# A pair of products ahead of the last logits, and a weight load that waits for the rows' stores

## What is computed

```python
u = rmsnorm(h, norm_ffn_g[i])                         # normalised rows
aff = softmax(einsum('nd,de->ne', xf, router_w))      # xf: the rows u; router's logits
gate, idx = lax.top_k(aff.T, cap)                     # each expert's 64 tokens
xs = xf[idx]                                          # its rows, gathered
hid = silu(einsum('ecd,edf->ecf', xs, w_gate)) * einsum('ecd,edf->ecf', xs, w_up)
out = einsum('ecf,efd->ecd', hid, w_down) * gate[..., None]
```

## Time and profile before

| what | value |
|---|---|
| executions | 1513.92, 1514.42, 1514.67 us (median 1514.42) |
| the profiled execution | 1513.21 us, of which the span is 1511.4 us |
| TensorE busy | 1496.6 us (99% of the span) |
| VectorE, ScalarE, GpSimd busy | 1335.3, 1283.8, 443.9 us |
| read from and written to memory | 473.70 and 20.97 MB, 327 GB/s over the span |
| granted TensorE clock, mean | 0.998 of full speed |

### The profile page before, as it was taken

One profiled execution on the slowest core, in us unless ns is written; L12 is line 12 of the kernel. 1 busy time (PEld: TensorE's weight loads), 2 busy tenths in 40 slices (PEclk: granted clock), 3 DMA queues, 4 the chain that ended last, 5 costly groups with the idle time before them and its releaser, 6 DMA issues.

```text
span 1511.4 us, 21957 instructions
## 1 busy us (share of the span) xinstructions
PE 1496.6 (99%) x7514; PEld 1212.0 (80%) x7514; DVE 1335.3 (88%) x1415; ACT 1283.8 (85%) x1611; POOL 443.9 (29%) x354
## 2 busy tenths in 40 slices
PE   9999999999999999999999999999999999999997
PEld 8888888878864888888888888888888888888876
DVE  7776887787864999999999999999999999999988
ACT  6777766676653799999999999999999999999997
POOL 0434203252222224232332423224232322520103
PEclk9999999999999999999999999999999999999999
DMA  9615447333575999999999999999999999999998
GB/s 351 210 71 179 150 166 267 98 126 126 188 260 217 399 420 393 416 401 398 410 403 410 394 407 401 396 412 397 409 392 396 413 397 407 397 410 382 391 394 345
DMA packets 156023, 498.57 MB, mean 330 GB/s; under 512 B 11008, under 2 KB 36736, under 8 KB 155968
## 3 DMA queue, kind: packets, MB, share of 16 engines
q1 hardware_dynamic: 144624, 461.54, 77.9%
q0 software_dynamic: 10048, 34.22, 7.4%
q10 hardware_dynamic: 1296, 2.10, 0.4%
HBM read 473.70 MB, written 20.97 MB: 327 GB/s over the span
## 4 chain that ended last, share of the span: by engine, by line
PE 82%; ACT 5%; DVE 5%; issue 3%; DMA 2%; POOL 2%; SPq 0%; POOLq 0%; ACTq 0%; DVEq 0%
PE ps L2124 71%; PE ps L2173 4%; PE ps L2180 2%; ACT w_high L1286 2%; POOL arena L746 2%; DVE w_rest L1437 1%; ACT arena L950 1%; PE ps L2442 1%; PE ps L2224 1%; DMA raw<-w_gate 1%; PE ps L2290 1%; DVE arena L1511 1%; ACT arena L1257 1%; DVE arena L1534 1%; DMA u_rows<-arena 1%
## 5 line engine op out<-in xcount | busy, mean ns | idle before, releaser
L1437 DVE TENSOR_TENSOR w_rest<-raw,w_high 128x2048 fp32r<-128x2048 f32 x212 | 479.9, 2294 | 36.9 <-ACT w_high L1286 25.1
L1286 ACT CAST w_high<-raw 128x2048 fp32r<-128x2048 f32 x184 | 352.1, 1915 | 17.6 <-PE ps L2124 14.7
L2124 PE MATMUL ps<-w_high,xt_high 128*128 128x512 f32 x984 | 305.2, 390 | 0.7 <-DVE w_rest L1437 0.6
L2124 PE MATMUL ps<-w_rest,xt_high 128*128 128x512 f32 x984 | 304.3, 389 | 0.0
L2124 PE MATMUL ps<-w_high,xt_rest 128*128 128x512 f32 x984 | 304.3, 389 | 0.0
L2124 PEld LDWEIGHTS ps<-w_high,xt_high 128*128 128x128 f32 x984 | 184.1, 188 | 41.6 <-DVE w_rest L1437 2.4
L1437 DVE TENSOR_TENSOR w_rest<-early,w_high 128x2048 fp32r<-128x2048 f32 x90 | 204.4, 2287 | 13.4 <-ACT w_high L1286 13.3
L2124 PEld LDWEIGHTS ps<-w_high,xt_rest 128*128 128x128 f32 x984 | 184.7, 188 | 38.5
L2124 PEld LDWEIGHTS ps<-w_rest,xt_high 128*128 128x128 f32 x984 | 184.7, 188 | 38.4
L1437 DVE TENSOR_TENSOR w_rest<-raw_more,w_high 128x2048 fp32r<-128x2048 f32 x92 | 206.0, 2275 | 4.7 <-ACT w_high L1286 4.7
L870 POOL DMA_INDIRECT h_rows<-xh,rows x15 | 109.2, 7280 | 303.8 <-ACT xh L1268 303.8
(11 more groups left out here) (323 smaller groups left out, 2471.3 us busy)
## 6 DMA issues: line engine op xcount, KB each, us to landing
raw<-w_down SPq DMA_DIRECT2D x64, 1024.0 KB, 9.1
raw<-w_gate SPq DMA_DIRECT2D x62, 1024.0 KB, 8.0
raw<-w_up SPq DMA_DIRECT2D x62, 1024.0 KB, 9.8
raw_more<-w_down SPq DMA_DIRECT2D x32, 1024.0 KB
early<-w_down SPq DMA_DIRECT2D x32, 1024.0 KB, 8.0
raw_more<-w_gate SPq DMA_DIRECT2D x31, 1024.0 KB
raw_more<-w_up SPq DMA_DIRECT2D x31, 1024.0 KB
early<-w_gate SPq DMA_DIRECT2D x31, 1024.0 KB, 9.9
```

The lines of the kernel that those rows point to most:

```text
L1286: nc.scalar.copy(w_high[:, i % SLOTS, :], src).then_inc(high_done, 1)
L1437: nc.vector.tensor_tensor(w_rest[:, j, :], src, w_high[:, j, :].bitcast(F32), ALU.subtract).then_inc(rest_done, 1)
L2124: done = nc.tensor.matmul(out, lhs, rhs, start=start and part == 0, stop=stop and part == 2)
```

## The change

Two edits. On TensorE, the pair of products for share 0 of piece 0 leaves its place behind `last_group` and is issued between the last `quarter_logits` and the last `logits` of trunk 1, with the waits that stood ahead of it. On SyncE, piece 1 of `load_second` waits for the stores of the normalised rows as well, a wait that piece 2 had; piece 2 keeps its wait for the gather.

```diff
@@ load_second(i), SyncE
                     sp.wait_ge(scaled, TILES * TRUNKS)
                     sp.wait_ge(h_out, 16 * TILES * TRUNKS)
+                    sp.wait_ge(u_out, 16 * TILES * TRUNKS)
                 elif i == 2:
 
-                    sp.wait_ge(u_out, 16 * TILES * TRUNKS)
                     sp.wait_ge(gathered, 16)
@@ last_group(b), TensorE
                 quarter_logits(b, 3)
                 if b + 1 < TRUNKS:
                     project_t(b + 1, None, "q0", pair_number(b + 1, "q", 0), KC // 2)
+                else:
+                    first_early_gate_up(b)
                 logits(b, 3)
@@ new
+            def first_early_gate_up(b):
+
+                pe.wait_ge(early_xt_done, 1)
+                wait_copied(pe, b, GROUPS - 1, "o6")
+                wait_copied(pe, b, GROUPS - 1, "o7")
+                early_gate_up(0, (0,))
@@ behind the groups, TensorE
-            pe.wait_ge(early_xt_done, 1)
-            wait_copied(pe, TRUNKS - 1, GROUPS - 1, "o6")
-            wait_copied(pe, TRUNKS - 1, GROUPS - 1, "o7")
-            early_gate_up(0)
+            early_gate_up(0, (1,))
             early_gate_up(1, (0,))
             turn_lists(1)
             early_gate_up(1, (1,))
```

## The result

The changed kernel takes 1516.56 us at the median of 22 executions (1514.17 to 1518.50, but for one at 1659.57, whose mean granted clock was 0.85 and which is left out of the ratio). The kernel before took 1513.97 us beside it (22 executions, 1513.41 to 1516.07). The ratio is 1.0014 (by the medians alone 1.0017), with a 95% interval of 1.0007 to 1.0020: the change makes the kernel slower, by 2.6 us at the medians. Forecast were 1513.8 us in a range that ended at 1515.4. The profiled execution of after took 1517.09 us (1515.2 of span), that of before 1513.21.

A forecast was written before the change was run, and what follows sets the result against it. TensorE, busy 1496.6 of 1511.4 us, was taken as the bound, so only its two waits (1.16 us) could yield. Rows 0.65 us earlier, 0.2 of it from the pair, made 1514.42 into 1513.8; range 1512.6 to 1515.4.

The forecast's parts named there:

- Part 1: Pair of products moved into TensorE's 0.46 us hole before the last logits: logits 0.55 us late, lists turned 0.2 us earlier.
- The stores' end: Stores of the normalised rows, freed of the w_up load, finish their last 0.33 MB in 0.8 us and signal at 455.3.
- The third rival: Stores' tail is slow for its own reason, landing near 457 even without the load; 1514.2 us, chance 0.07.
- The gather's releaser: First expert's gather is released by the row numbers at 456.6, not by the stores, and starts 0.5 us later at 457.1.
- The gather's delay: The w_up load overlaps the first expert's gather by about 1 us and delays it by 0.3 us.
- a row and a rule: Gather beside load: profile row shows a queue's tail hardly moving (0.06 MB beside 0.75); skill's rule says queues alternate by packet.
- the sum: Load issued near 455.4, gather started 457.1, TensorE on the rows 0.65 us earlier: 1513.21 becomes 1512.6, at the median 1513.8.
- The second rival: The w_up load starves the first expert's gather: 0.3 us slower (1514.7), at worst 3.6 us (1518.1); chance 0.12.
- Hidden work: ScalarE's cast of the w_up load slips 1 to 4 us, hidden because its products come 23 us behind.
- the likeliest case: TensorE takes up the gathered rows at 461.4 instead of 462.05; gain 0.65 us, between 0.3 and 1.05, chance 0.55.
- The base of the sum: Median of the measured executions of the kernel before, 1514.42 us, from which the gain of 0.65 was subtracted.
- the ends: Outcomes bounding the whole-kernel forecast: 1513.3 us with a gain of 1.05, 1514.7 us with a loss of 0.3.

The follow-up runs named there:

- e8: Changed kernel, with the w_up load waiting until GpSimd has asked for the gather, instead of for the stores; 1517.50 us, ratio 1.0029 to the kernel before.
- e4: Changed kernel plus four pairs of unused products on TensorE just ahead of its wait for the gathered rows; 1514.32 us, ratio 1.0007 to the kernel before.
- e5: The changed kernel itself, run again beside other runs on the same chip; 1516.04 us, ratio 1.0017 to the kernel before.
- e2: Kernel before, with only the w_up load's added wait for the stores of normalised rows, the pair left in place; 1515.29 us, ratio 1.0011.
- e9: Changed kernel, with the 1 MB w_up load issued as four 256 KB loads one behind the other; 1516.89 us, ratio 1.0021 to the kernel before.
- e3: Changed kernel, with the w_up load waiting for the gather instead of the stores; 1513.08 us, ratio 1.0000 to the kernel before.
- e1: Changed kernel, with the pair moved but the w_up load given back its old wait; 1513.07 us, ratio 0.9998 to the kernel before.
- e6: Changed kernel, with the second half of the w_up load waiting for the gather to land; 1513.56 us, ratio 1.0002 to the kernel before.
- e7: Kernel before, with the w_up load waiting for the gather and the pair left in place; 1512.96 us, ratio 0.9998.

## Why the prediction was wrong

- **Part 1 was right.** The logits stand 1.73 us behind the quarter logits (1.81 was worked out), VectorE's scaling now waits for them, for 0.18 us, and the lists gain 0.2 us. This is VectorE's timeline, to set against the earlier trace rows:

```profile
441.52 0.22 DVE L1896 TENSOR_TENSOR lg<-ps,rstd 128x64 f32<-128x64 f32 x1 [0.18 <-PE ps L2489]
...
457.36 0.15 DVE L1838 TENSOR_TENSOR first_rows_at<-topt 64x1 uint32<-64x1 f32 x1
```

- **The stores' end was mis-sized by 1.5 us.** The step took the last 0.33 MB of the stores at their full rate, 0.8 us. Measured from the last store's issue, they land 9.46 us behind it instead of 10.02, where the prediction had about 8.0 (455.3 less 447.29). The row of 0.06 MB in 2 us beside the load was read as a queue starved by a flood. By its share it was one engine at the end of its work, which a rate of all sixteen does not tell. The third rival, that the tail is slow for its own reason, given 0.07, was right here. The stores and the row numbers now come together (457.43 and 457.51), so there was no time to win between them, and the load is issued only 0.9 us ahead of the gather's start, when the sum had 1.7.

- **The gather's releaser was right, its start nearly:** the row numbers, and 0.82 us behind them where 0.5 was taken.

- **The gather's delay is the step that failed:** 0.3 us was taken, 1.71 measured (5.54 less 3.83). I had a row and a rule against each other there and went by the rule, with turns so short that a quarter of a megabyte is slowed by its own size at most. The Trainium skill ("DMA: Bandwidth & Descriptors", Queues, rings and completion order) has each engine take turns between its queues packet by packet, and counts some 9 to 17 descriptors, at most 64, to a packet. The tail of the stores in before agrees with turns, and with the shortest (the 0.235 us above). For this gather beside one whole load the trace does not agree with turns as the prediction took them: its first packet moves at 461.80, when 495 of the load's 512 have started, and e8 shows it for a gather asked for within 0.12 us of the load. If the page's descriptors are the packets that the trace lists, an engine's share of the load (32, of 512 over sixteen engines) could be one long turn; but the same load let the stores' packets in one by one, so that alone would not explain it. The second rival, the starved gather, given 0.12, is what happened. Its price was worked out as 0.3 to 3.6 us; in the traces the rows come 1.08 us later than before (24.73 less 23.65). The row that I set against the rule was itself misread (the point on the stores); it only happened to point the right way.

- **The clock is missing in the sum.** A wait was priced at its own length. Here 1.98 us of standing still drew 1.70 more after them. The prediction read the clock before the change (1.00 in the earlier trace rows) and did not ask what a longer wait would do to it. e4 shows that it is the idleness: with products in the wait, the clock stays. The Trainium skill ("TensorE: Matmul & The Clock Gate", What's actually happening) says that TensorE's clock is lowered after idleness. The traces of after and e5 agree (in after 1.00 through the wait, 0.50 behind it); behind the waits of e2, e8 and e9 the clock stayed at 1.00.

- **Hidden work was right.** ScalarE's cast of the load now waits 5.97 us for it and ends at 464.48, far ahead of the products that need it, and e3's load, 5 us later still, costs nothing. The loop passes every microsecond on: 1026.5 to 1026.8 us from its first product to the end, in all of them.

So the likeliest case (a gain of 0.65) failed at the gather, and the range failed at the clock: with the starved gather alone the time would have been about 1514.9 (1513.97 and the 0.97 of e4), inside it, and the clock's 1.7, which more than half of the executions seem to pay (13 of 21 took 1516.2 us or more), went past its end at 1515.4. The base of the sum, 1514.42 from three executions, lay 0.45 above the 1513.97 of 22, and the ends and the 0.6 that the range names give 1512.7 to 1515.3; neither changes the outcome. Of the causes, that the load holds up the gather (e3 against e5, e1 against e2) and that the idleness costs the clock (e4 against e5) are shown. Not settled is what in the DMA engines makes the gather wait. No run had a load that reached the engines second while the gather moved, so being the first to arrive may be what counts. A single 8 KB packet of an instruction queue moves within 0.07 us of the gather's first data in eight of the eleven traces, and is as late as they are beside the load; but in e4, e9 and e6 the gather's first data come 0.2, 0.4 and 0.5 us ahead of that packet, so the gather does not wait for it there. Nor is it settled why the clock falls in some executions of one kernel and not in others (last section).

## What to carry to other kernels

Before a load is moved off one transfer, look at which transfer it is moved onto: a small gather that TensorE waits for should have no big load issued in the last microsecond or so ahead of it (here 0.1 to 1.3 us), and e3 and e7 show that such a load can simply wait for the gather when its user has time. Where a queue's last bytes trickle, read the trickle's share of the engines (6% is one of sixteen) before it is called starved. And price a new wait of TensorE with the clock behind it: here, in the profiled execution, 2 us of waiting cost 3.7.

## What was not expected of the hardware

- A gather of 256 KB on GpSimd's queue got no data until SyncE's load of 1 MB was through or nearly so (455 to 506 of its 512 packets had started): it landed 6.29 to 6.44 us behind the load's issue in five kernels, 5.43 with half a load, and 3.82 to 3.88 us behind its own start when no load stood ahead of its data. The same load in four pieces let the gather in, and both were slower (7.41 us behind the first piece's issue).
- The stores of the normalised rows end in a chain of single 4 KB packets, one every 0.155 us for about 1 us, by their share (6.0%) the work of one of the sixteen DMA engines, and 0.5 us more pass to the release of SyncE.
- A single wait of TensorE in a busy stretch can halve its granted clock soon after, for 3.4 us, at 1.7 us. It did so in the profiled executions with 1.98 and 1.90 us of wait (after, e5) and not in those with 1.47, 2.62 and 3.03 us (e2, e8, e9), so the wait's length does not decide it alone. What else does is left open here.
